# Splitting the expert weight loads of a mixture-of-experts layer over two DMA queues, SyncE's and GpSimd's

## The reference, cut to what matters

```python
logits = (h @ w_r + b_r).astype(jnp.float32)
top_v, top_i = lax.top_k(logits, TOP_K)
top_w = jax.nn.softmax(top_v, axis=-1)
...
for e in range(N_EXPERTS):
    z = h @ w1[e] + b1[e]
    glu = jnp.minimum(z[:, :D_FF], SWIGLU_LIMIT)
    lin = jnp.clip(z[:, D_FF:], -SWIGLU_LIMIT, SWIGLU_LIMIT)
    act = glu * jax.nn.sigmoid(SWIGLU_ALPHA * glu) * (lin + 1)
    out = out + comb[:, e:e + 1] * (act @ w2[e] + b2[e])
```

## Time and profile before

| what | value |
|---|---|
| median of 3 runs | 1319.1 us (1318.95 to 1322.22) |
| the profiled execution's own time | 1316.12 us |
| its span | 1314.4 us |
| TensorE busy | 1260.8 us, 96% |
| VectorE, ScalarE, GpSimd busy | 353.2, 216.4 and 28.0 us |
| moved by DMA | 476.01 MB, mean 362 GB/s |
| granted TensorE clock, mean | 0.994 |

### The profile page before, as it was taken

The page is one execution under the profiler, slowest core; times in us unless marked ns, Lnnn a source line. Parts: engine busy times, 40 slices in busy tenths (PEclk is TensorE's granted clock), DMA queues, the critical chain, the costliest instruction groups (busy, mean ns, idle before and its releaser), DMA issues.

```text
span 1314.4 us, 13725 instructions
## 1 busy us (share of the span) xinstructions
PE 1260.8 (96%) x5616; PEld 543.5 (41%) x5616; DVE 353.2 (27%) x623; ACT 216.4 (16%) x358; POOL 28.0 (2%) x74
## 2 busy tenths in 40 slices
PE   4999999899999999999999999999999999999995
PEld 2444678778543333333333333333333333333321
DVE  2647777421251211112111112111121111211112
ACT  3155641030120111001110011110011100101001
POOL 1000000000000000000000000000000000000000
PEclk9999999999999999999999999999999999999999
DMA  9632469877469999999999999999999999999994
GB/s 352 239 112 96 144 200 388 292 294 287 155 263 387 429 427 428 427 427 427 427 429 428 427 427 428 416 424 429 427 427 427 429 428 427 427 427 429 427 426 176
DMA packets 70926, 476.01 MB, mean 362 GB/s; under 512 B 5872, under 2 KB 39856, under 8 KB 43216
## 3 DMA queue, kind: packets, MB, share of 16 engines
q1 hardware_dynamic: 66480, 455.81, 84.0%
q0 software_dynamic: 2848, 18.88, 3.7%
q10 hardware_dynamic: 1536, 0.46, 0.2%
HBM read 474.07 MB, written 1.05 MB: 361 GB/s over the span
## 4 chain that ended last, share of the span: by engine, by line
PE 74%; DMA 17%; ACT 4%; DVE 3%; issue 1%; SPq 0%; DVEq 0%; ACTq 0%
PE bank L743 28%; PE bank L754 15%; DMA arena<-in_exp_w 13%; PE bank L649 9%; PE bank L721 4%; PE bank L765 4%; DMA arena<-in_w_in 3%; PE bank L638 2%; PE bank L579 2%; PE bank L556 2%; PE bank L730 2%; PE bank L808 1%; PE bank L611 1%; ACT arena L907 1%; DMA arena<-in_w_mod 1%
## 5 line engine op out<-in xcount | busy, mean ns | idle before, releaser
L743 PE MATMUL bank<-arena,temps 128*64 128x512 f32 x2112 | 463.1, 594 | 10.5 <-DMA arena<-in_exp_w 10.0
L743 PEld LDWEIGHTS bank<-arena,temps 128*64 128x64 f32 x2112 | 148.5, 137 | 322.4 <-issue 300.7
L754 PE MATMUL bank<-arena,temps 128*64 128x512 f32 x1056 | 233.9, 595 | 0.6 <-DVE temps L1399 0.6
L1392 DVE TENSOR_SCALAR temps<-bank 128x512 f32<-128x512 f32 x33 | 22.8, 691 | 667.5 <-PE bank L743 667.5
L754 PEld LDWEIGHTS bank<-arena,temps 128*64 128x64 f32 x1056 | 72.7, 137 | 138.4 <-issue 132.1
L649 PE MATMUL bank<-arena 128*128 128x256 f32 x512 | 111.6, 379 | 3.6 <-DMA arena<-in_w_in 2.8
L649 PEld LDWEIGHTS bank<-arena 128*128 128x128 f32 x512 | 97.1, 190 | 19.2 <-issue 5.1
L997 ACT ACTIVATE temps<-temps 128x512 f32<-128x512 f32 x33 | 20.8, 629 | 507.9 <-DVE temps L1392 507.9
L765 PE MATMUL bank<-temps,hot 64*128 64x512 f32 x264 | 65.6, 615 | 0.8 <-ACT temps L1005 0.8
L721 PE MATMUL bank<-vtokb,hot 128*64 128x512 f32 x264 | 65.4, 617 | 0.3 <-DVE hot L1245 0.3
L638 PE MATMUL bank<-arena 128*128 128x512 f32 x128 | 57.4, 606 | 2.4 <-DMA arena<-in_w_in 2.4
(11 more groups left out here) (244 smaller groups left out, 797.8 us busy)
## 6 DMA issues: line engine op xcount, KB each, us to landing
arena<-in_exp_w SPq DMA_DIRECT2D x192, 2048.0 KB, 24.3
arena<-in_w_in SPq DMA_DIRECT2D x20, 1024.0 KB, 6.3
arena<-in_w_mod POOLq DMA_DIRECT2D x16, 1024.0 KB, 7.7
arena<-in_w_mod SPq DMA_DIRECT2D x8, 1024.0 KB, 16.0
arena<-in_w_pool_proj SPq DMA_DIRECT2D x4, 1024.0 KB, 5.1
arena<-in_w_rnn_proj SPq DMA_DIRECT2D x4, 1024.0 KB, 6.2
arena<-in_w_out SPq DMA_DIRECT2D x4, 1024.0 KB, 10.2
arena<-in_lru_wa SPq DMA_DIRECT2D x8, 256.0 KB, 3.4
```

The source lines that it names most:

```text
L743: last = mm(psum[4 + q][h * SLOTS:(h + 1) * SLOTS, :], xg[:, k // 4, k % 4, :], w1_at[s][:, r, o:o + HALF], start=False, stop=(k == KT - 1))
L754: last = mm(psum[6][h * SLOTS:(h + 1) * SLOTS, :], actT[:, c, r, :], w2_at[s][:, r, h * HALF:(h + 1) * HALF], start=(c == 0 and r == 0), s ...
L1392: v.tensor_scalar(glu, psum[4][:, :], LIMIT, None, ALU.min).then_inc(glu_ready, 1)
```

## The change

The loads of the second matrix (c = 4 and 5) are issued by GpSimd from its own software queue, except those of the first item, which SP still issues on a pair of semaphores `early_landed`. SP issues c = 0 to 3 only. GpSimd waits for the same counts of `w_used` as SP did for those loads, and it does so after the bias copy for the same item. The landing semaphores are split into `first_landed` and `second_landed`, one of each per slot, and `landed_at` counts the landings of like loads in a slot. Slots, the order within each kind and all arithmetic stay.

```diff
@@ def landed_at(i, c):
+            n = load_no(i, c)
+            like = sum(1 for m in range(n + 1) if m % WSLOTS == n % WSLOTS and (m % CPI < 4) == (c < 4) and (c < 4 or m >= CPI))
             if isinstance(i, int):
-                return 16 * (load_no(i, c) // WSLOTS + 1)
-            return i * 16 + 16 * ((LAST + c) // WSLOTS + 1 - FIXED)
+                return 16 * like
+            return i * 16 + 16 * (like - FIXED)
@@ block.sync
             def load_expert(q, e, c):
                 s = (q * CPI + c) % WSLOTS
-                sp.dma_start((w1_at if c < 4 else w2_at)[s], expert_src(e, c)).then_inc(expert_landed[s], 16)
+                if c < 4:
+                    sp.dma_start(w1_at[s], expert_src(e, c)).then_inc(first_landed[s], 16)
+                else:
+                    sp.dma_start(w2_at[s], expert_src(e, c)).then_inc(early_landed[c - 4], 16)
...
-                for c in range(CPI):
+                for c in range(4):
                     n = q * CPI + c - WSLOTS
                     if n >= 0:
                         sp.wait_ge(w_used, place_done(n // CPI) * CPI + n % CPI + 1)
...
             with sp.Fori(NP - 1, last_item + 1) as i:
-                for c in range(CPI):
+                for c in range(4):
                     sp.wait_ge(w_used, (i - 1) * CPI + (c + 1))
                     load_expert(E - 2, e, c)
@@ block.gpsimd
+            def load_second(q, e, c):
+                s = (q * CPI + c) % WSLOTS
+                pool.dma_start(w2_at[s], expert_src(e, c)).then_inc(second_landed[s], 16)
...
             for i in range(FIXED):
                 pool.wait_ge(w_used, i * CPI + 1)
...
+                bias_rows_of(e)
+                if i + 1 != TWICE + 1 and i + 1 < NP - 1:
+                    q = place_of(i + 1)
+                    for c in range(4, CPI):
+                        n = q * CPI + c - WSLOTS
+                        pool.wait_ge(w_used, place_done(n // CPI) * CPI + n % CPI + 1)
+                        load_second(q, e, c)
...
             with pool.Fori(FIXED, last_item) as i:
                 pool.wait_ge(w_used, i * CPI + 1)
...
+                for c in range(4, CPI):
+                    pool.wait_ge(w_used, i * CPI + (c + 1))
+                    load_second(E - 2, e, c)
@@ block.tensor
-                    pe.wait_ge(expert_landed[s], landed_at(i, c))
+                    pe.wait_ge(first_landed[s], landed_at(i, c))
...
-                    pe.wait_ge(expert_landed[s], landed_at(i, 4 + c))
+                    if isinstance(i, int) and i == 0:
+                        pe.wait_ge(early_landed[c], 16)
+                    else:
+                        pe.wait_ge(second_landed[s], landed_at(i, 4 + c))
```

More of the change, by code:

```diff
@@ L225, in build @@
         ring_landed = [sem(f"ring_landed{r}") for r in range(RING)]
-        expert_landed = [sem(f"expert_landed{n}") for n in range(WSLOTS)]
+        first_landed = [sem(f"first_landed{n}") for n in range(WSLOTS)]
+        early_landed = [sem(f"early_landed{n}") for n in range(2)]
+        second_landed = [sem(f"second_landed{n}") for n in range(WSLOTS)]
         vecs_landed, tokens_landed, late_landed = sem("vecs_landed"), sem("tokens_landed"), sem("late_landed")
@@ L512, in _ @@
                 pool.wait_ge(w_used, i * CPI + 1)
-                if i + 1 < FETCHED:
-                    bias_rows_of(i + 1)
-                else:
+                e = i + 1
+                if i + 1 >= FETCHED:
                     if i + 1 == FETCHED:
                         pool.wait_ge(items_ready, 1)
-                    bias_rows_of(pool.value_load(tabE[0:1, i + 1:i + 2], min_val=0, max_val=E - 1))
+                    e = pool.value_load(tabE[0:1, i + 1:i + 2], min_val=0, max_val=E - 1)
+                bias_rows_of(e)
[5 more added lines that the diff above has]
+                        load_second(q, e, c)
             last_item = pool.value_load(more[0:1, 0:1], min_val=0, max_val=MORE - 1) + (NP - 1)
@@ L521, in _ @@
                 pool.wait_ge(w_used, i * CPI + 1)
-                bias_rows_of(pool.value_load(tabE[0:1, ds(i + 1, 1)], min_val=0, max_val=E - 1))
+                e = pool.value_load(tabE[0:1, ds(i + 1, 1)], min_val=0, max_val=E - 1)
+                bias_rows_of(e)
+                for c in range(4, CPI):
+                    pool.wait_ge(w_used, i * CPI + (c + 1))
+                    load_second(E - 2, e, c)
         @block.tensor
```

## The result

The changed kernel takes 1335.99 us (median of 6 runs, 1329.09 to 1337.79), before 1319.28 us: a ratio of 1.0114, 95% interval 1.0095 to 1.0133. Run again on another occasion it took 1336.01 us (5 runs, 1335.72 to 1338.44), ratio 1.014, interval 1.0119 to 1.0162. Both times the median is 16.7 us higher (the ratios given are not those of the medians, which are 1.0127 both times). The prediction was 1335, +16.2.

What follows compares the result with a forecast made beforehand. DMA landings of first-matrix loads were taken to bound items 13 to 15 and the end, TensorE between. 9 + 9.8 - 2.6 = 16.2 us on 1319.1 gave 1335.3 us; own range 1327 to 1342, 8 in 10 1320 to 1345.

Steps and rivals of the forecast that it cites:

- What bounds the kernel: Last first-matrix load's landing sets the time at items 13 to 15 and at the end; TensorE, 27.36 us an item, between.
- No cost for issuing, waiting and semaphores: GpSimd's 62 extra issues, some 1.1 us an item, its new waits and the split semaphores cost nothing.
- Packets alternate one for one, 16 KB in both queues: DMA engines alternate packets between queues, so GpSimd's gets half the bandwidth and its two loads finish in 19.6 us.
- Step 1: Items 13 to 15: two overtaking loads delay c = 3 by 9.8 us, item 15's to 822.3, item 16 to 839.3.
- Step 2: Handover at item 16: DMA runs dry, next load issued 843.2, landed 850.9; DMA 9.1 us later, taken as 9.
- Step 3: The end: item 31's c = 3 lands at 1274.8, item 32's c = 3 starts at 1302.2, 16.2 us later than before.
- The sum: Whole kernel: 9 + 9.8 - 2.6 = 16.2 us slower, the 2.6 from item 32 running without a wait.
- Two of the signs: First-matrix loads over 40 us at the ceiling; forecast wrong if the rate over 420 to 1290 us is not 427 GB/s.
- Rival (a): Second matrix comes last, its queue getting a fifth of the bytes with 4 KB packets: 2.7 us earlier, 1316.4; chance 0.09.
- The sum for 8 KB runs: If GpSimd's runs were cut to 8 KB, a third share, two loads through in 29.5 us; loss stays near 13.
- Rival (b): More bandwidth: two queues fill packet gaps by 2% or more, all weight waits go, 12.8 us less, 1306; chance 0.05.
- Rival (c): Software queue slower, 398 instead of 427 GB/s for its 62 loads: 22 us on top of the forecast, 1357; chance 0.08.

Runs made afterwards that it cites:

- the split with 8 KB runs: The changed kernel with the second matrix in runs of 8 KB instead of 16 KB; 1341.21 us, 1323.38 with the same runs in one queue.
- the one with 4 KB runs: The changed kernel with the second matrix in runs of 4 KB on GpSimd's queue, SP's packets still 16 KB; 1366.57 us, ratio 1.0354 to the kernel before.
- its yardstick: The kernel before, one queue, with the second matrix in runs of 4 KB instead of 16 KB; 1331.67 us, ratio 1.0103 to the kernel before.

## Why the prediction was right, step by step

*What bounds the kernel.* Right: the overtaking costs where DMA sets the pace, and between those stretches TensorE does. Items 16 to 24 run at 27.36 us each as before; from item 24 on there are waits again, where before had the first at item 29.

*No cost for issuing, waiting and semaphores.* Right. GpSimd issued 183 loads in the kernel with one software queue at no measurable loss.

*Packets alternate one for one, 16 KB in both queues.* Right. The size is shown by the 144 packets a load. The alternation was inferred from one stretch of 6 us with 8 KB and 1 KB packets; the kernels of the study show it at all three shares, in stretches in which both queues have work: 801:804 of the kernel after (16 KB in both), 716:720 of the split with 8 KB runs, and 752:756 of the one with 4 KB runs. A row has packets, MB and share of the 16 engines.

```profile
q0 software_dynamic: 42, 0.69, 55.0%
q1 hardware_dynamic: 40, 0.57, 45.0%
...
q1 hardware_dynamic: 78, 1.07, 62.7%
q0 software_dynamic: 78, 0.64, 38.2%
...
q1 hardware_dynamic: 96, 1.31, 77.4%
q0 software_dynamic: 96, 0.39, 24.1%
```

Landing in the new queue took 15.5 us, where the step said 10 to 25.

*Step 1,* c = 3 of item 15 at 822.3 and item 16 at 839.3: measured 822.3 and 839.3 (less the 3.6 of the front). *Step 2,* issue at 843.2 and 7.7 us to land: measured 843.2 and 7.8. The gap was forecast at 837 to 845 and stands there. *Step 3,* c = 3 of item 31 at 1274.8: measured 1275.7. Of the 0.9 us between them 0.6 is the standstill: by DMA's bytes it was 9.6 us, where the sum had 9.1 and took 9. Item 32 then runs without a wait for weights, the 2.6 us are given back, and the last second map is 17.1 instead of 16.2 us later.

*The sum* is 16.2 for 16.7 (first set) and 16.7 (second) by the medians, and for 17.1 and 16.9 by the single places. That the mechanism is right is shown by the places; that the medians agree within 0.5 us is partly luck, since their interval alone is 2.5 us to either side. The predicted end of the profiled execution, 1332.3, is 4.4 below the measured 1336.72, of which 3.6 is the front.

*Two of the signs* in the prediction were wrong, though the forecast was not. First-matrix loads were to take over 40 us at the ceiling; they took 34.7 to 37.8 us from 1100 to 1200 and 39.1 at most from 600 to 700. Why they stay under the ceiling of before was not looked into. And the forecast was to be wrong if the rate from 420 to 1290 us was not 427: it is 422 in the kernel after. That sign contradicts the forecast's own standstill, which takes 9 of these 870 us away; outside of it the rate is 427.

*What was wrong besides* is in the part on bounds and rivals. Rival (a) said that with a fifth of the bandwidth for the second matrix the kernel would be 2.7 us faster. Its mechanism was looked at only at the last load of each DMA-bound stretch; the kernel with 4 KB runs shows that the second matrix starves long before, and it is 34.9 us slower than its yardstick. Even at the end the 2.7 could not be had: c = 3 of the last item cannot land earlier than two loads before the end of all. The sum for 8 KB runs was given as near 13; measured 17.8. So the 0.09 given to it stood on a mechanism that the kernel with 4 KB runs refutes. Rival (b) fell: 427 GB/s in both kernels from 850 to 1290 us, and the Trainium skill's rule that several issuing engines bring no bandwidth (DMA: Bandwidth & Descriptors, Rules for kernel authors) agrees with that number. Rival (c) fell with the kernel on one software queue.

## What to carry to other kernels

In this kernel loads that are used in a fixed order belong in one queue in that order, since DMA is the bound at the end: the second queue added no bandwidth (427 GB/s with one and with two), it decided who is served first, by packet size. Bytes served ahead of need took the place of those that were needed, whichever of the two streams got too much: 16.7 us with the second matrix at a half, 34.9 with it at a fifth. And look for DMA standing still under a busy engine: with this ring of slots the gap came when TensorE was late at a point where DMA had caught up, and it was paid for at the next place where DMA is the bound.

## What the runs showed of the hardware that I had not expected

A software queue fed by GpSimd carried 183 loads of 2 MB at the full 427 GB/s of the hardware queue. Its issue took 0.53 us for 128 runs of 16 KB, 0.70 us for 256 runs of 8 KB and 0.74 us for 512 runs of 4 KB, so four times the runs cost 0.21 us more. Runs of 4 KB in a third of the bytes lowered the rate from 427 to 421 GB/s. An estimate from these rates for the 402.7 MB of expert weights is 13.4 us; that kernel is 12.4 us slower than the one before.
